# Windowed attention inside a decoder-layer kernel: heads paired over the key groups, values held stationary, output written with features on partitions

## The reference

```
scores = einsum('bnqhgd,bnkhd->bnhgqk', qb, kband) * (d ** -0.5)
scores = where(valid, scores, -inf)            # k_pos <= q_pos, q_pos - k_pos < 128
m = maximum(max(scores, -1), sink)
p = exp(scores - m)
denom = sum(p, -1) + exp(sink - m)
out = einsum('bnhgqk,bnkhd->bnqhgd', p / denom, vband)
y_b = out.reshape(b, s, 16 * 64) @ w_swa_out
```

## Time and profile before

| | us |
|---|---|
| median of 3 runs | 1220.1 |
| lowest, highest | 1219.74, 1222.08 |
| profiled execution, device time | 1219.12 |
| its span, first to last instruction | 1217.3 |
| TensorE busy | 1128.4 |
| VectorE busy | 361.6 |
| ScalarE busy | 267.6 |
| GpSimd busy | 143.2 |

### The profile page before, as it was taken

One profiled execution on the slowest core, in us unless ns is written; L12 is line 12 of the kernel. 1 busy time (PEld: TensorE's weight loads), 2 busy tenths in 40 slices (PEclk: granted clock), 3 DMA queues, 4 the chain that ended last, 5 costly groups with the idle time before them and its releaser, 6 DMA issues.

```text
span 1217.3 us, 17311 instructions
## 1 busy us (share of the span) xinstructions
PE 1128.4 (93%) x7218; PEld 558.1 (46%) x7218; DVE 361.6 (30%) x622; ACT 267.6 (22%) x405; POOL 143.2 (12%) x100
## 2 busy tenths in 40 slices
PE   7999989998999999999999999999999999999886
PEld 5988989985343333333333333333333333333332
DVE  5878743955122111111111111111111111111112
ACT  5465736232111111111111111111111111111112
POOL 6545543541000000000000000000000000000000
PEclk9999999998999999999999999999999999999999
DMA  7544326777999999999999999999999999999995
GB/s 303 207 166 156 109 100 235 297 292 292 429 369 429 427 429 426 427 429 430 427 428 429 429 427 429 429 427 429 429 429 427 429 429 428 427 430 429 427 428 209
DMA packets 35826, 448.14 MB, mean 368 GB/s; under 512 B 4160, under 2 KB 4288, under 8 KB 6576
## 3 DMA queue, kind: packets, MB, share of 16 engines
q1 hardware_dynamic: 34992, 445.99, 88.0%
q0 software_dynamic: 368, 1.24, 0.3%
q10 hardware_dynamic: 432, 0.42, 0.1%
HBM read 446.58 MB, written 1.05 MB: 368 GB/s over the span
## 4 chain that ended last, share of the span: by engine, by line
PE 47%; DMA 46%; DVE 3%; issue 2%; POOL 1%; ACT 1%; SPq 0%; DVEq 0%; ACTq 0%
DMA ring<-wexp 45%; PE PS L822 23%; PE PS L560 13%; PE PS L815 3%; PE PS L807 2%; PE PS L879 1%; DMA EXT<-be 1%; DMA ring<-wblk 1%; PE PS L658 1%; PE PS L684 1%; DVE EXT L1197 1%; POOL slot_R L492 1%; PE PS L874 1%; PE PS L671 0%; PE PS L595 0%
## 5 line engine op out<-in xcount | busy, mean ns | idle before, releaser
L822 PE MATMUL PS<-ring,SQ 128*64 128x512 f32 x2016 | 455.1, 596 | 61.9 <-DMA ring<-wexp 61.6
L822 PEld LDWEIGHTS PS<-ring,SQ 128*64 128x64 f32 x2016 | 138.1, 136 | 353.5 <-issue 227.5
L822 PE MATMUL PS<-ring,PTG 128*64 128x512 f32 x1024 | 226.8, 595 | 0.0
L822 PEld LDWEIGHTS PS<-ring,PTG 128*64 128x64 f32 x1024 | 70.7, 137 | 152.2 <-issue 133.2
L492 POOL TENSOR_TENSOR slot_R<-ring,slot_R 128x512 fp32r<-128x512 f32 (+1 forms) x80 | 122.6, 1563 | 102.6 <-ACT slot_R L923 102.6
L1593 DVE TENSOR_SCALAR SQ<-PS 128x512 f32<-128x512 f32 x32 | 22.1, 691 | 365.3 <-PE PS L822 365.3
L1107 ACT ACTIVATE SQ<-SQ 128x512 f32<-128x512 f32 x32 | 20.2, 630 | 501.8 <-DVE SQ L1593 501.8
L1584 DVE TENSOR_TENSOR PTG<-TAB,GR 128x128 bf16<-128x128 f32 x32 | 9.3, 292 | 333.8 <-PE PS L867 333.8
L560 PE MATMUL PS<-slot_R 128*128 128x256 f32 (+1 forms) x296 | 93.0, 314 | 0.0
L923 ACT ACTIVATE slot_R<-ring 128x2048 fp32r<-128x2048 f32 (+1 forms) x38 | 71.7, 1889 | 40.2 <-DMA ring<-wblk 21.3
L560 PE MATMUL PS<-HT_R,slot_R 128*128 128x256 f32 x400 | 74.9, 289 | 3.5 <-ACT EXT L961 3.3
(11 more groups left out here) (266 smaller groups left out, 956.8 us busy)
## 6 DMA issues: line engine op xcount, KB each, us to landing
ring<-wexp SPq DMA_DIRECT2D x190, 2048.0 KB, 33.4
ring<-wblk SPq DMA_DIRECT2D x36, 1024.0 KB, 4.8
EXT<-wexp SPq DMA_DIRECT2D x2, 2048.0 KB, 8.8
BRW<-brow SPq DMA_DIRECT2D x7, 256.0 KB, 5.1
ring<-wskv SPq DMA_DIRECT2D x2, 768.0 KB, 11.6
EXT<-x SPq DMA_DIRECT2D x2, 512.0 KB, 4.3
out<-EXT SPq DMA_DIRECT2D x3, 256.0 KB, 2.0
EXT<-gfin POOLq DMA_DIRECT2D x1, 512.0 KB, 8.1
```

The costliest lines, as they stand in the source:

```text
L822: last = mm(PS[g * SLOTS:(g + 1) * SLOTS, b, :], lhsT, rhs[:, g * 512:(g + 1) * 512], start=start, stop=stop)
```

## The change

- Groups take two heads of either key group: heads 2g, 2g+1 and 8+2g, 8+2g+1. The host permutes the query columns, their biases, the sinks and the rows of the output projection. Keys lie on partitions 0 to 63 and 64 to 127 once, so two key transposes are left of four, and the rotated keys are written once, not twice.
- `values` holds the 64 value features of a key head stationary and streams the probabilities of two heads, 256 columns, past them. The two key heads write PSUM partitions 0 to 63 and 64 to 127. The output has features on partitions.
- The denominators are then no scalars for a partition any more. VectorE's new `swa_denominator` writes each reciprocal 64 times (128x256), TensorE transposes these in two steps at the end of `values`, ScalarE's new `swa_rb` copies them from PSUM to `KTT[:, 1]`, and VectorE's `swa_out` multiplies after that copy.
- `attention_t` and its waits go. ScalarE rounds the result with one copy and VectorE subtracts in one operation, behind `rest(24)`; TensorE waits for both ahead of block swao0.

```
             def values(n):
...
+                for st in range(i + 1):
+                    for kv in range(2):
+                        mm(PS[kv * HD:(kv + 1) * HD, 3, 0:2 * P], KVRAW[:, st, P + kv * HD:P + (kv + 1) * HD],
+                           PTS[:, n % 2, kv, 2 * st * P:2 * (st + 1) * P], start=(st == 0), stop=(st == i))
+                pe.wait_ge(sw_rd, n + 1)
+                for j in range(2):
+                    last = nc.tensor.transpose(PS[:, 3, (2 + j) * P:(3 + j) * P], KD[:, j, P:2 * P], ident)
                 last.then_inc(sw_o, 1)
...
-            dense(10, {(0, 1): [attention_t]})
+            dense(10)
...
+            def swa_rb(n):
+                act.wait_ge(sw_o, n + 1)
+                if n:
+                    act.wait_ge(sw_out, n)
+                fn(KTT[:, 1, :], PS[:, 3, 2 * P:4 * P], ACT.Copy).then_inc(sw_rb, 1)
...
             for n in range(NGRP + 1):
+                if n >= 2:
+                    swa_rb(n - 2)
                 if 0 <= n - 1:
                     swa_pt(n - 1)
...
+            swa_rb(NGRP - 1)
             act.wait_ge(gr_ready, 3)
...
+            act.wait_ge(sw_out, NGRP)
+            fn(OB2[0], OB_RAW, ACT.Copy).then_inc(obt_hi, 1)
...
+            def swa_denominator(n):
+                q = n % 2
+                dve.wait_ge(sw_exp, n + 1)
+                link(v.tensor_tensor(S_DEN[q], S_SUM[q], S_ES[q], ALU.add))
+                v.reciprocal(KD[:, :, P:2 * P].rearrange("p j (v d) -> p j v d", v=2),
+                             S_DEN[q].rearrange("p (v j) -> p j v", v=2).unsqueeze(3).broadcast_to([P, 2, 2, HD])).then_inc(sw_rd, 1)
 
             def swa_out(n):
                 i, g4 = n // (NGRP // TT), n % (NGRP // TT)
...
+                dve.wait_ge(sw_rb, n + 1)
+                v.tensor_tensor(OB_RAW[:, 2 * g4:2 * g4 + 2, i * P:(i + 1) * P],
+                                PS[:, 3, 0:2 * P].rearrange("p (j t) -> p j t", j=2),
+                                KTT[:, 1, :].rearrange("p (j t) -> p j t", j=2), ALU.mult).then_inc(sw_out, 1)
...
                 if n < NGRP:
                     swa_mask(n)
+                if 0 <= n - 1 < NGRP:
+                    swa_denominator(n - 1)
                 if evac:
                     token_major(u, dst[:, 1, c:c + BW], BW)
...
-            rest_t(OB2, obt_full, obt_lo)
             rest(24)
+            dve.wait_ge(obt_hi, 1)
+            v.tensor_tensor(OB2[1], OB_RAW, OB2[0].bitcast(F32), ALU.subtract).then_inc(obt_lo, 1)
```

More of the change, by code:

```diff
@@ L194, in program @@
         S_DEN = [small(50 + 4 * b, 4) for b in range(2)]
-        S_RD = [small(58 + 4 * b, 4) for b in range(2)]
         S_GS, S_GVAR, S_GSD, S_GRS = small(66, 8), small(74, 8), small(82, 8), small(90, 8)
@@ L222, in program @@
         OB2 = (feature(SQ_R), feature(SQR_R))
+        OB_RAW = feature(SQR)
         OA2 = (feature(GV_R), feature(GR_R))
@@ L636, in _ @@
             pe.wait_ge(krot_ready, TT)
[L637 to L640, removed]
+            for i in range(TT):
+                last = nc.tensor.transpose(PS[:, 3, i * P:(i + 1) * P], KD[:, i, 0:P], ident)
             last.then_inc(kt_full, 1)
@@ L655, in scores @@
                 for hh in range(HG):
[L656 to L660, removed]
+                    kv, j = hh % 2, hh // 2
+                    rows = slice(kv * HD, (kv + 1) * HD)
+                    last = mm(PS[:, 4 + kv, j * SEQ:j * SEQ + ns], qT[rows, 2 * g4 + j, i * P:(i + 1) * P],
+                              KTT[rows, 0, 0:ns], start=True, stop=True)
                 last.then_inc(sw_s, 1)
@@ L670, in probs_t @@
                     for st in range(i + 1):
-                        last = nc.tensor.transpose(PS[:, 6 + hh // 2, (2 * (hh % 2) + st) * P:(2 * (hh % 2) + st + 1) * P],
-                                                   SS[:, n % 2, hh, st * P:(st + 1) * P], ident)
+                        c = (2 * st + hh % 2) * P
+                        last = nc.tensor.transpose(PS[:, 6 + hh // 2, c:c + P], SS[:, n % 2, hh, st * P:(st + 1) * P], ident)
                 last.then_inc(sw_t, 1)
@@ L756, in _ @@
             for i in range(13, NB - 1):
+                if BLOCKS[i] == "swao0":
+                    pe.wait_ge(obt_hi, 1)
+                    pe.wait_ge(obt_lo, 1)
                 dense(i)
@@ L1227, in rotate @@
                 link(v.tensor_tensor(t2, src[:, :, 1, :], s, ALU.mult))
-                for d in dst:
-                    last = v.tensor_tensor(d[:, :, 0, :], t1, t2, ALU.subtract)
-                link(last)
+                link(v.tensor_tensor(dst[:, :, 0, :], t1, t2, ALU.subtract))
                 v.tensor_tensor(t1, src[:, :, 1, :], c, ALU.mult)
                 link(v.tensor_tensor(t2, src[:, :, 0, :], s, ALU.mult))
-                for d in dst:
-                    last = v.tensor_tensor(d[:, :, 1, :], t1, t2, ALU.add)
-                last.then_inc(done, 1)
+                v.tensor_tensor(dst[:, :, 1, :], t1, t2, ALU.add).then_inc(done, 1)
                 dve.wait_ge(done, i + 1)
@@ L1309, in _ @@
                 evacuated(dve, 4 + i)
-                kd = KD[:, i, :].rearrange("p (h c x d) -> p h c x d", h=2, c=2, x=2)
                 rotate(KVRAW[:, i, 0:P].rearrange("p (h x d) -> p h x d", h=2, x=2),
-                       [kd[:, :, c] for c in range(2)], 2, i, krot_ready)
+                       KD[:, i, 0:P].rearrange("p (h x d) -> p h x d", h=2, x=2), 2, i, krot_ready)
             dve.wait_ge(z_ready, GH)
@@ L1319, in _ @@
             dve.wait_ge(kt_full, 1)
-            v.tensor_copy(KTT[:].rearrange("p g t -> p (g t)"), bk(3)).then_inc(kt_ready, 1)
+            v.tensor_copy(KTT[:, 0, :], bk(3, SEQ)).then_inc(kt_ready, 1)
             for a in range(2, 4):
@@ L1345, in swa_pt @@
             def swa_pt(n):
-                i = n // (NGRP // TT)
+                w = 2 * (n // (NGRP // TT) + 1) * P
                 dve.wait_ge(sw_t, n + 1)
-                v.tensor_copy(PTS[:, n % 2, 2:4, 0:(i + 1) * P],
-                              PS[:, 7, :].rearrange("p (h s) -> p h s", h=2)[:, :, 0:(i + 1) * P]).then_inc(sw_ptV, 1)
+                v.tensor_copy(PTS[:, n % 2, 1, 0:w], PS[:, 7, 0:w]).then_inc(sw_ptV, 1)
+            def swa_denominator(n):
[4 more added lines that the diff above has]
+                             S_DEN[q].rearrange("p (v j) -> p j v", v=2).unsqueeze(3).broadcast_to([P, 2, 2, HD])).then_inc(sw_rd, 1)
             def swa_out(n):
                 i, g4 = n // (NGRP // TT), n % (NGRP // TT)
[L1353 to L1364, removed]
+                dve.wait_ge(sw_rb, n + 1)
+                v.tensor_tensor(OB_RAW[:, 2 * g4:2 * g4 + 2, i * P:(i + 1) * P],
+                                PS[:, 3, 0:2 * P].rearrange("p (j t) -> p j t", j=2),
+                                KTT[:, 1, :].rearrange("p (j t) -> p j t", j=2), ALU.mult).then_inc(sw_out, 1)
             dve.wait_ge(row_in, 16)
@@ L1640, in units, with head_pairs @@
         return w.reshape(2, KH, P, -1).transpose(0, 2, 1, 3).reshape(2, P, -1)
+    def head_pairs(a):
+        return a.reshape(2, QH // 2, HD, -1).transpose(1, 0, 2, 3).reshape(QH * HD, -1)
+    sq = slice(at["sq"], at["sq"] + QH * HD)
+    w_in, b_in = w_in.copy(), b_in.copy()
+    w_in[:, sq] = head_pairs(w_in[:, sq].T).T
+    b_in[sq] = head_pairs(b_in[sq])[:, 0]
     def columns(name):
@@ L1644, in columns @@
             w = f[{"gl": "w_gla_out", "sw": "w_swa_out", "wo": "w_out"}[name[:2]]][0]
+            if name[:2] == "sw":
+                w = head_pairs(w)
             n = int(name[-1]) * BW
```

24 lines of the change are left out of this document (7 added, 17 removed).

## The result

| | median us | lowest, highest |
|---|---|---|
| before, run beside it | 1219.97 | 1219.74, 1222.08 |
| after | 1229.99 | 1229.22, 1230.67 |

The ratio is 1.008, its 95% interval 1.0065 to 1.0095: 10.0 us more. The profiled execution took 1229.22 us for a span of 1227.4, 10.1 more than before. The forecast was 6.4 more, and up to 11.4 within its range (1231.5 less 1220.1).

A forecast was written before the change was run, and what follows sets the result against it. TensorE's entry into the expert loop sets the weight stream and the end. TensorE returns to block 10 8.1 us later, less 1.75 for removed transposes: +6.4, median 1226.5 us, range 1222 to 1231.5.

The forecast's parts named there:

- rival C: Attention: stalls between groups lower TensorE's clock, or more small VectorE operations are held up; 1229 to 1231 us, chance 0.15.
- denominator step: VectorE behind each mask: sum plus wide reciprocal, 2.4 us, eight times; TensorE's transposes of the reciprocals wait for it.
- What bounds the kernel: Whole kernel: expert-weight stream starts a fixed time after TensorE enters the expert loop; a TensorE microsecond moves the end by one.
- The wide reciprocal: VectorE, per group: a reciprocal of 128x256 takes 2.2 us, several times a simple pass.
- Rival A: VectorE's wide reciprocal costs only a simple pass, 0.42 us; end +2.5 us, 1222.6, chance 0.10.
- The new loop through ScalarE: Attention: output multiply waits for ScalarE's late copy; mask intervals 8.65, 8.55, 11.4 and 11.4 us.
- Mask 3 to 4: Attention, VectorE's own queue: mask, denominators, bias add, rest and decay products, output and probabilities sum to 9.2 us.
- mask(2): VectorE's mask of group 2 begins 1.0 us later than before: 2.4 less 1.4, one step held up.
- Mask(7) to TensorE's return: End of attention to block 10: 21.3 us in sum, TensorE back at 166.4, 8.1 later than before.
- All after it hangs on TensorE: After block 10: expert chunks, bias transfer and refill wait move along with TensorE, at no further cost.
- TensorE's products: Attention values: passes on different array halves overlap; 1.06 us per two-block group instead of 1.73, 0.45 less with two transposes.
- Rival B: Attention: the new waits are hidden and TensorE's loop stays longest; -3.3 us, 1216.8, chance 0.05.

The follow-up runs named there:

- e1: Changed kernel with VectorE taking the reciprocal of four elements and copying it to 64 places: +6.2 us against the kernel before, ratio 1.0051.
- e4: Kernel before plus a ScalarE copy of 128x256 from PSUM after each group's values, which the output multiply waits for: +5.2 us, ratio 1.0044.
- e11: Changed kernel with four-element reciprocal, VectorE copying the transposed reciprocals, and last gate product ahead of last attention output: -6.5 us against the kernel before, ratio 0.9953.
- e9: Kernel before with only the last gate product's two operations moved ahead of the last attention output: -6.1 us, ratio 0.995.
- e12: Changed kernel with four-element reciprocal, VectorE copying transposed reciprocals, gate product first, expert biases behind multiplications of blocks 13 and 14: -9.1 us against the kernel before, ratio 0.9924.
- e5: Changed kernel with four-element reciprocal written out by a copy, and VectorE copying the transposed reciprocals itself: +0.3 us against the kernel before, ratio 1.0007.

## Why the prediction was right, and where its terms were off

The time came out in the range but 3.5 us above the forecast median (1226.5), and inside the 1229 to 1231 that the prediction gave to rival C at 0.15. (From C's 2 to 4 us on the forecast follows 1228.5 to 1230.5.) The path was the forecast's, through ScalarE's copy and the denominator step; a part of C, more held-up VectorE steps, came on top.

**What bounds the kernel.** Right. The DMA gap moved by 10 us with TensorE's entry, and the stream behind it kept its length.

**The wide reciprocal.** Forecast 2.2 us, measured 1.753; group by form, changed kernel:

```profile
L1353 DVE RECIPROCAL EXT<-SM 128x256 f32<-128x256 f32 x8 | 14.0, 1753 | 0.3
```

With 179 ns for four elements that is (1753 - 179)/252 = 6.2 ns per element. Rival A's simple pass of 0.42 fell. The prediction's estimate of 2.1, worked out from the repeat count of 8 that the Trainium skill (VectorE: DVE Perf Modes, section First, the fixed hardware budget) gives, was too high as well: the measurement decides. The denominator step was 1.9, not 2.4, which alone would have brought the time under the forecast. Taking the wide reciprocal away, as in e1, is worth 3.8 us (10.0 less 6.2). TensorE's waits for it sum to 7.7 us, in five of the slots, where the prediction named near 10 and a wait in each.

**The new loop through ScalarE.** Right, and the forecast's main part: intervals 8.70 (forecast 8.65), 8.78 (8.55), 10.87 and 11.76 (11.4 each), with the output multiply released by line 998. e4 shows it by itself.

**Mask 3 to 4.** The step that failed most: 10.52, forecast 9.2. The price of the two decay products, 1.13 us together, came from a stretch in which they ran free; they were held up to 1.78 and 1.77. The mis-sized term is this one, about 1.1 us twice, in part made good by the cheaper reciprocal. With mask(2) 0.46 later than forecast, where another such step took 2.30 instead of 1.22 (line 1284), this is nearly all of the 1.9 us by which mask(7) was missed. Rival C named such hold-ups, with 2 to 4 us.

**Mask(7) to TensorE's return.** 21.36, forecast 21.3, which is luck: from the last output multiply at 160.98 to TensorE's return it took 7.4 and not 5.9, since the weight rest and both gate products (lines 1403 and 1405, before 1407 and 1409) were held up, and the part ahead of it took 13.9 and not 15.4. TensorE's idle time before its return was 5.0, not 3. The clock behind it cost what it had cost: the granted clock was 0.57 over the 4 us from 168 on, and 0.57 over those from 158 on before.

**"All after it hangs on TensorE", cost 0.** This step was wrong by 2.2 us. The bias chain starts from TensorE, as argued, but it doesn't merely move along: a transfer that lands 1.2 later and a bias step that meets GpSimd made TensorE's waits there 4.2 instead of 2.0. e11 against e9 shows the same loss without any delay ahead of it, and in e12 these waits go with the steps that were moved.

In sum: 2.1 at the return (10.16 against 8.1), 2.2 in the bias chain, less 0.2 as the removed transposes saved 1.9 and not 1.75, and less 0.3 between the loop's entry (+10.4) and the end (+10.1), make 3.8, the difference between +6.4 and +10.1 but for rounding.

**TensorE's products.** Two passes on the two halves overlap: values of a two-block group are one link of 1.01 us in the chain, `159.15 1.01 PE PS L680 x8`, forecast 1.06, before 1.73. Rival B would have turned this into a gain. e5 shows that even with both added steps undone it would have been within 0.2%, because the bias steps take it.

**Rival C's clock.** After the wait of 3.39 us the 8 transposes took 1.91 and the 8 score passes 1.50, where they take 0.88 and 1.06 at full clock. The granted clock was 0.56 and 0.59 there, so 1.7 us went to it:

```profile
120.00:122.00 2.00, 1.46 (x7) 1.41 (x8) 1.03 (x2) 2.00 (x6) 0.00 (x0) 0.56 0.36 152
122.00:124.00 2.00, 2.00 (x13) 1.52 (x11) 1.02 (x2) 1.49 (x3) 1.22 (x1) 0.59 0.00 0
```

It happened in one slot. The loop from mask to mask felt at most 0.47 us of it, the wait of mask(5) for these score passes. What it cost in the end was not measured.

## What to carry to other kernels

A step added to an engine's in-order list costs what it delays behind it: an unread 1.75 us step for each of eight groups cost 7.9 us (in its profiled run 6.5) and a 0.37 us copy behind another engine's long list 5.2, so look for who waits behind the place where the step goes, and for the other engine's port that the delay moves it onto. Before rebuilding what an engine computes, look at the waits of the bounding engine that don't depend on it: moving two operations forward in one list gave 6.1 us (in the profiled runs 4.5), giving the bias steps a later place about 2 more, and the rebuilt attention by itself nothing that could be measured. A gain in front of a wait is only kept if that wait doesn't grow, which the time at which TensorE passes each later station shows.

## What the hardware showed beyond expectation

- A reciprocal costs 6.2 ns for each element of a partition (128x256 in 1.75 us), four times a simple pass of that size (0.42).
- VectorE steps with two SBUF inputs are prolonged by up to 1.1 us, whatever their size, when they meet a GpSimd part: 128x1024 1.22 to 2.31, 128x512 0.68 to 1.78, 128x4 0.15 to 1.25. Where GpSimd's part is nearly over it is less: line 1340's 128x4 step, 0.16 us when free, took 0.82 in one slot of the changed kernel and ended at 127.81, GpSimd's four parts at 127.80. Casts to bf16 with one input are held up as well (32x2048: 1.22 before, 2.21 in the changed kernel, line 1199).
- A TensorE wait of 3.3 to 3.7 us delayed the next station by 5.0 to 5.5 us; 1.8 of it is the granted clock of 0.94 in that window. Shorter waits are followed by a lower clock in some executions and not in others: behind 1.75 us in e5 (at 220.26) the granted clock was 0.63 and 0.51 in two stretches of 2 us, behind 1.84 and 2.38 us in the changed kernel (230.54 and 244.69) it was 1.00.
- The small transfer of the biases lands about 1 to 2 us later after its issue in each of the nine kernels without the 16 transposes of block 10. This stays unexplained.
